# One core, streamed fp32 weights: reciprocal root rows inside a tile, two mixer tails in a new order, mLSTM gates as a full tile

## The chip, the core and the metric

The kernel runs on one core of a Trainium2 chip. The metric is the device time of one execution in microseconds (us); below it is the median of the runs shown. The profile is of one further execution.

The engines are called PE (TensorE, matmuls), DVE (VectorE), ACT (ScalarE), POOL (GpSimd) and SP (SyncE, which here only issues loads).

## The reference

A sequence of 256 tokens with 1024 features goes through six layers. The first two (`hybrid_layer`) project once, run three mixers side by side and project back. The other four are what the change is mostly about:

```python
def swiglu(x, w_gu, w_down):
    g, u = jnp.split(x @ w_gu, 2, axis=-1)
    return (jax.nn.silu(g) * u) @ w_down
...
for layer in range(4):
    g = norm_gains[layer]
    h = x + 0.5 * swiglu(rmsnorm_2(x, g[0]), w_ffn_gu[layer, 0], w_ffn_down[layer, 0])
    xn = rmsnorm_2(h, g[1])
    mix = hgrn2_mixer / mlstm_mixer / swa_mixer / hgrn2_mixer   # layer 0, 1, 2, 3
    h = h + mix(xn)
    h = h + 0.5 * swiglu(rmsnorm_2(h, g[2]), w_ffn_gu[layer, 1], w_ffn_down[layer, 1])
    gate = jax.nn.sigmoid(rmsnorm_2(h, g[3]) @ w_ple_gate[layer])
    x = h + gate * (p[layer] @ w_ple_proj[layer])
```

`rmsnorm_2` divides a token by the root of the mean of its squares and multiplies with a gain. An HGRN mixer has 8 heads of 128 and ends in: norm of each head, times `silu(og)`, times `w_out`. In layer 0 the lower bound `lb` of its forget gate is 0, in layer 3 it is not. The mLSTM mixer has 4 heads of 256 values; 8 gate columns `x @ w_if` (four input, four forget gates) go through `15 * tanh(gates / 15)` and a log-sigmoid; it ends in a norm of each head, times `sigmoid(og)`, times `w_out`. All is fp32.

## The kernel before

**Layout.** x lies transposed, features on the partitions: `x_res` is 128 x 8 tiles x 256 tokens. A product gives one PSUM tile of 128 outputs x 256 tokens.

**The stream of weights.** All weights come as 781 chunks of 128 x 1024 fp32 (`w_raw`), one for one output tile over all 8 feature tiles. SP issues their loads (L80) into 4 buffers. ACT rounds a chunk to the high part `w_hi` (L90, `hi_for`), DVE takes the difference, `w_lo` (L98, `lo_for`); both have 6 buffers. PE waits for a chunk (`wait_chunk`) and then makes three matmuls per feature tile j: L138 (high x high), L139 (high x `w_lo`), L144 (`xn_lo` x high), 24 in a tile. x is split the same way into `xn_hi` (L204 on ACT) and `xn_lo` (L209 on DVE).

**A norm without waiting.** The division by the root is put behind the product. While PE already multiplies the unscaled x, sums of squares are made (L366 on PE, `sum_squares`), their mean goes to SBUF (L379, ACT), POOL takes the power -1/2 (L393), PE spreads the result over 128 partitions by two transposes (L404, in `rstd_rows`), and DVE copies that to SBUF (L412, `take_rstd`). Only then can DVE scale the finished tiles (L536, L690, L982, L987) and free their PSUM banks. A section starts with a stretch in which two tiles run side by side, first all products with `xn_hi`, then those with `xn_lo` ("low phase"). `rstd_rows` stands in the third or fourth tile.

**PSUM.** Banks: `ps_gu` 0 and 1, four of `ps_acc`, `ps_sum`, `ps_misc`.

**Sections.** `ffn`: gate and up tiles in turn, `h = silu(g) * u` split by L519 and L545, then down products into `ps_acc`. `ple`: gate and projection. `project`: the input tiles of a mixer. `OutProjection`: y is split pair by pair (`split_hi` L1177, `split_lo` L1187); its first four output tiles are computed side by side as y comes (`place` gives their banks, so the four chunks are all needed early), the other four after that. Its `finish` adds each tile to x (L1271), and splits and squares the new x for the next section (L204, L209, L217; folds of squares L244, L248).

**The tails.** In `hgrn` the 8 head outputs lie in `ps_acc`; `head_norm` takes squares, their sums over partitions on PE into `ps_gu`, Ln and Exp, then DVE multiplies (L2355, L2360). Between them four gate tiles are projected into `ps_sum` and `ps_misc`, read by L982. `end_mixer` then gives the output product the banks `ps_gu` 0, `ps_gu` 1, `ps_sum`, `ps_misc`: the two last of them are free only after L982 has read the last two gate tiles. `mlstm` does the same with L3193, L3212, L3223, the sigmoid L3231 and its table load L3253.

**The forget gate with a bound** (`bounded`, layer 3): POOL does two operations for each of four heads (L2732, L2733), twice; the decays wait for the last.

**mLSTM gates.** The 8 gate columns are a first tile of another form: the weights' 8 columns are the moving side, tokens on the partitions (L153, L154, L158, 128 x 8 results, 48 matmuls), side by side with the first query tile. `gate_steps` places their small operations between the next tiles.

The order on each engine is the order in which the program writes it; there is no scheduler.

## Time and profile before

| | us |
|---|---|
| median of 3 runs | 2593.26 |
| lowest, highest | 2592.62, 2598.38 |
| the profiled execution, device time | 2591.68 |
| its span in the trace | 2589.7 |
| PE busy in it | 2515.2 |
| DVE, ACT, POOL busy | 1724.2, 1322.9, 97.3 |

Between the span and the time of the same execution lie 2.0 us. A bracket behind a row of a timeline, [2.41 <-DVE x_res L1271], is the time for which the engine had nothing to do before this instruction, and what ended it. The granted clock is given as a share of full speed. A tile of 24 matmuls at full clock takes 2.88 us, 0.12 us from one start to the next, though each matmul is listed with 0.28 us, since they overlap.

### The profile page before, as it was taken

To read this page: it belongs to the slowest core of one execution; us is meant where nothing else is said; L and a number is where in the kernel's file an instruction comes from. 1 tells how busy PE (TensorE), PEld (TensorE's weight loads), DVE (VectorE), ACT (ScalarE), POOL (GpSimd) and SP (SyncE) were. 2 spreads that over 40 slices of the span, in tenths; PEclk is the share of its full clock that TensorE was granted. 3 is DMA by queue.
4 is the path that set the end of the run, shared out by engine and by line. 5 is a ranking of instruction groups with operands and counts; after the bars stand their busy time and mean duration, and the time that the engine had idled before them with its cause. 6 is when DMAs were issued, how large, how long until landed. Compare 5 with 4: busy or idle time off the path is not lost.

```text
span 2589.7 us, 51722 instructions
## 1 busy us (share of the span) xinstructions
PE 2515.2 (97%) x20424; PEld 2478.8 (96%) x20424; DVE 1724.2 (67%) x2417; ACT 1322.9 (51%) x2019; POOL 97.3 (4%) x103
## 2 busy tenths in 40 slices
PE   7999999999999999999999999998999999999999
PEld 7999999999999999999899999987999999999999
DVE  7768757568665576566666675676666755767656
ACT  5745645446554464444444554465445544655444
POOL 1010010001100000000000000000000000220000
PEclk9999999999999999999999999999999999999999
DMA  7305306554355545555365555532555555435553
GB/s 259 123 34 171 123 33 212 186 179 163 122 171 186 181 162 190 183 158 175 115 198 182 172 178 186 180 125 87 188 182 167 187 185 182 161 122 171 180 186 122
DMA packets 115233, 418.85 MB, mean 162 GB/s; under 512 B 12816, under 2 KB 13968, under 8 KB 114832
## 3 DMA queue, kind: packets, MB, share of 16 engines
q1 hardware_dynamic: 114240, 413.10, 48.8%
q8 instruction: 108, 1.77, 0.3%
q0 software_dynamic: 560, 2.10, 0.3%
q10 hardware_dynamic: 288, 1.57, 0.2%
q14 instruction: 37, 0.30, 0.0%
HBM read 414.62 MB, written 2.10 MB: 161 GB/s over the span
## 4 chain that ended last, share of the span: by engine, by line
PE 82%; DVE 11%; ACT 3%; issue 2%; POOL 1%; DMA 0%; SPq 0%; DVEq 0%; ACTq 0%
PE ps_gu L138 15%; PE ps_gu L144 15%; PE ps_gu L139 15%; PE ps_acc L138 8%; PE ps_acc L144 8%; PE ps_acc L139 8%; DVE w_lo L98 3%; PE ps_acc L2590 1%; ACT w_hi L90 1%; PE ps_misc L138 1%; PE ps_acc L2148 1%; PE ps_misc L139 1%; PE ps_misc L144 1%; PE ps_sum L366 1%; DVE arena L1593 1%
## 5 line engine op out<-in xcount | busy, mean ns | idle before, releaser
L98 DVE TENSOR_TENSOR w_lo<-w_raw,w_hi 128x1024 fp32r<-128x1024 f32 x781 | 953.0, 1225 | 451.7 <-ACT w_hi L90 451.6
L138 PE MATMUL ps_gu<-xn_hi,w_hi 128*128 128x256 f32 x3840 | 1087.5, 286 | 25.7 <-DVE w_lo L98 12.1
L139 PE MATMUL ps_gu<-xn_hi,w_lo 128*128 128x256 f32 x3840 | 1077.9, 284 | 0.0
L144 PE MATMUL ps_gu<-xn_lo,w_hi 128*128 128x256 f32 x3840 | 1041.3, 284 | 0.0
L90 ACT ACTIVATE w_hi<-w_raw 128x1024 fp32r<-128x1024 f32 x781 | 819.9, 1054 | 417.4 <-PE ps_gu L144 305.3
L138 PEld LDWEIGHTS ps_gu<-xn_hi,w_hi 128*128 128x128 f32 x3840 | 738.7, 192 | 32.2 <-DVE w_lo L98 12.1
L139 PEld LDWEIGHTS ps_gu<-xn_hi,w_lo 128*128 128x128 f32 x3840 | 739.3, 193 | 0.3
L144 PEld LDWEIGHTS ps_gu<-xn_lo,w_hi 128*128 128x128 f32 x3840 | 717.1, 192 | 0.0
L138 PE MATMUL ps_acc<-h_hi,w_hi 128*128 128x256 f32 x1496 | 420.3, 281 | 1.2 <-DVE h_lo L545 1.2
L144 PE MATMUL ps_acc<-h_lo,w_hi 128*128 128x256 f32 x1496 | 420.3, 281 | 0.0
L139 PE MATMUL ps_acc<-h_hi,w_lo 128*128 128x256 f32 x1496 | 416.4, 278 | 0.0
L515 ACT ACTIVATE silu<-ps_gu 128x256 f32<-128x256 f32 x176 | 67.6, 384 | 456.0 <-DVE ps_gu L536 456.0
L138 PEld LDWEIGHTS ps_acc<-h_hi,w_hi 128*128 128x128 f32 x1496 | 281.9, 188 | 2.8 <-DVE h_lo L545 2.8
L139 PEld LDWEIGHTS ps_acc<-h_hi,w_lo 128*128 128x128 f32 x1496 | 281.9, 188 | 0.0
L144 PEld LDWEIGHTS ps_acc<-h_lo,w_hi 128*128 128x128 f32 x1496 | 280.7, 188 | 0.0
L536 DVE TENSOR_TENSOR ps_gu<-ps_gu,rstd 128x512 f32<-128x512 f32 x176 | 123.0, 699 | 85.9 <-PE ps_gu L144 85.6
L540 DVE TENSOR_TENSOR h<-silu,ps_gu 128x256 f32<-128x256 f32 x176 | 74.2, 421 | 89.9 <-ACT silu L515 89.9
L393 POOL TENSOR_TENSOR rstd_columns<-mean_square_columns,powers 128x2 f32<-128x2 f32 x17 | 14.2, 836 | 2029.6 <-ACT mean_square_columns L379 2029.6
L545 DVE TENSOR_TENSOR h_lo<-h,h_hi 128x256 fp32r<-128x256 f32 x176 | 73.7, 419 | 7.7 <-ACT h_hi L519 7.7
L519 ACT ACTIVATE h_hi<-h 128x256 fp32r<-128x256 f32 x176 | 71.8, 408 | 7.8 <-DVE h L540 7.8
L138 PE MATMUL ps_misc<-xn_hi,w_hi 128*128 128x256 f32 x232 | 67.6, 291 | 5.2 <-issue 3.2
L204 ACT ACTIVATE xn_hi<-x_res,vec 128x256 fp32r<-128x256 f32 x136 | 61.7, 497 | 21.2 <-DVE x_res L576 13.6
(452 smaller groups left out, 2751.2 us busy)
## 6 DMA issues: line engine op xcount, KB each, us to landing
w_raw<-in_w_dram SPq DMA_DIRECT2D x781, 512.0 KB, 4.1
const<-in_const_dram SPq DMA_DIRECT2D x1, 1280.0 KB, 10.3
x_res<-in_x_dram SPq DMA_DIRECT2D x2, 512.0 KB, 5.8
distance_rows<-arena POOLq DMA_DIRECT2D x1, 1024.0 KB, 6.3
p_all<-distance_rows POOLq DMA_DIRECT2D x2, 512.0 KB, 6.1
p_all<-in_p_dram ACTq DMA_DIRECT2D x1, 1024.0 KB, 6.6
...
```

The costliest lines, as they stand in the source:

```text
L90: act.activation(self.w_hi[:, s, :], self.w_raw[:, r, :], ACT.Copy).then_inc(self.w_hi_ready.sem, 1)
L98: dve.tensor_tensor(self.w_lo[:, s, :], self.w_raw[:, c % NR, :], self.w_hi[:, s, :], ALU.subtract)\
L138: pe.matmul(out, self.w_hi[:, s, j0:j0 + width], rhs_hi, start=start, stop=False, skip_group_check=True)
L139: pe.matmul(out, self.w_lo[:, s, j0:j0 + width], rhs_hi, start=False, stop=False, skip_group_check=True)
L144: return pe.matmul(out, self.w_hi[:, s, j0:j0 + width], rhs_lo, start=False, stop=last, skip_group_check=True)
L204: act.activation(self.hi[:, m, :], self.k.x[:, m, :], ACT.Copy, scale=self.gain[:, m:m + 1])\
L366: mm = pe.matmul(k.ps_sum[:, tt:tt + 1], k.xn[:, m, tt * P:(tt + 1) * P], k.ones[:, 0:1], start=(m == 0 and tt == 0), stop=(m == tiles[-1] ...
L515: act.activation(k.s[:, t % 2, :], k.ps_gu[t % 2][:, 0:S], ACT.Silu).then_inc(silu.sem, 1)
L519: act.activation(k.h_hi[:, t % 2, :], k.h[:, t % 2, :], ACT.Copy).then_inc(hh.sem, 1)
L536: dve.tensor_tensor(gu, gu, k.rstd[:, :].unsqueeze(1).to_broadcast([P, 2, S]), ALU.mult).then_inc(sc.sem, 1)
L540: dve.tensor_tensor(k.h[:, t % 2, :], k.s[:, t % 2, :], k.ps_gu[t % 2][:, S:2 * S], ALU.mult)\
L545: dve.tensor_tensor(k.h_lo[:, t % 2, :], k.h[:, t % 2, :], k.h_hi[:, t % 2, :], ALU.subtract)\
```

## The change

It has eight parts.

A. `ffn`: the two transposes of `rstd_rows` stand inside tile t = 1, n = 0, behind its fifth of eight products, not behind the whole tile. One kind of ffn (`inner`, before the first of the four layers) keeps its place.
B. `ple`: they stand ahead of tile m = 2, not behind its fifth product.
C. `project` with its own root, and the first tile of a `first_layer`: behind product j = 2, not j = 4.
D. `OutProjection.finish`: DVE adds the last two x tiles before it makes the last two `w_lo`; ACT likewise splits the last x tiles before the last `w_hi`.
E. `bounded`: the fourth head's two operations go from POOL to DVE.
F. `hgrn`'s tail is written out in `hgrn`; the gate tiles alternate with the norms in another order, and output tiles 2 and 3 go to the two `ps_acc` banks whose heads were normed first.
G. `mlstm`: the gate columns are a tile of the ordinary form (24 matmuls, 256 columns wide, padded weights). DVE scales it, then PE turns it by two transposes (`turn_gates`) in the fifth tile; `gate_steps` come one tile later.
H. `mlstm`'s tail: the sigmoid's table is loaded earlier, the last two gate tiles are read later (`later=True`), one chunk is split at a place of its own, and output tiles 2 and 3 go to the banks of the first two heads.

`head_norm`, which the first two layers still use, keeps only the case with two outputs.

```diff
@@ ffn
+                    if t == 1 and n == 0 and j == (KD - 1 if k.inner else 4):
+                        rstd_rows(k, pe)
                 mm.then_inc(k.chunk_done.sem, 1)
-                if t == 1 and n == 0:
-                    rstd_rows(k, pe)
@@ ple
+        rstd_rows(k, pe, n)
         for m in range(2, KD):
...
-                if m == 2 and j == 4:
-                    rstd_rows(k, pe, n)
@@ project
-                if with_rstd and t == 3 and j == 4:
+                if with_rstd and t == 3 and j == 2:
                     rstd_rows(k, pe)
+                if within and t == len(tiles) - 1 and j == 2:
+                    within(pe)
@@ OutProjection.finish, vector engine
+                if 0 < t < KD - 2:
                     k.lo_for(dve, c0 + t)
-                for n in {5: [0], 6: [1]}.get(t, []):
-                    nxt.fold_step(dve, n)
+                if t == 5:
+                    fold(dve, 0)
+            k.lo_for(dve, c0 + KD - 2)
+            fold(dve, 1)
             nxt.split_lo(dve, KD - 1)
-            nxt.fold_step(dve, 2)
+            fold(dve, 2)
+            k.lo_for(dve, c0 + KD - 1)
@@ first_layer
-            if j == 4:
+            if j == 2:
                 rstd_rows(k, pe)
@@ hgrn, bounded
-            for n in range(4):
+            for n in range(3):
                 pool.wait_ge(*at[n])
+                ins = factors(pool, 4 * g + n)
+        @block.vector
+        def _(dve):
+            dve.wait_ge(*at[3])
+            dve.wait_ge(*made("forget_ready"))
+            factors(dve, 4 * g + 3).then_inc(*up("forgets_ready"))
@@ hgrn, tail
+    sums(0)
+    sums(1)
+    for j in range(2):
+        normed(j)
+        gated(j, early)
+    g4 = gate_tile(4, k.ps_sum, side[0])
+    out.split_hi(0)
+    sums(2)
+    sums(3)
+    out.split_lo(0)
+    out.split_hi(1)
+    out.split_lo(1)
+    g5 = gate_tile(5, k.ps_misc, side[1])
+    gate_at = last_silu(2, [g4, g5])
+    normed(2)
+    normed(3)
+    g6 = gate_tile(6, k.ps_sum, [g4])
+    gated(2, gate_at)
+    g7 = gate_tile(7, k.ps_misc, [g5])
+    out.split_hi(2)
+    gate_at = last_silu(3, [g6, g7])
+    out.split_lo(2)
+    gated(3, gate_at)
+    out.split(3)
+    end_mixer(k, out, [(k.ps_acc[:, order[j], :], [norm_at[j]]) for j in range(2)])
@@ mlstm, gates
+    def turn_gates(pe):
+        pe.wait_ge(*gates_read)
+        for w in side:
+            pe.wait_ge(*w)
+        for tt in range(TT):
+            mm = pe.transpose(k.ps_misc[:, tt * P:(tt + 1) * P], den[:, tt * P:(tt + 1) * P], k.ident)
+        mm.then_inc(turned.sem, 1)
...
-    project(k, [("mul", True, 8, gates[:, 0:2, :])] + [("mul", False, P, m(q, h)) for h in range(H)],
-            first=True, with_rstd=True, beside=gate_steps)
+    project(k, [("mul", False, P, m(den, 0))] + [("mul", False, P, m(q, h)) for h in range(H)],
+            first=True, with_rstd=True, beside=gate_steps, within=turn_gates)
@@ mlstm, tail
+    g6 = gate_tile(6, k.ps_sum, g4, hi_done=True, later=True)
     normed(2, root1)
+    block.vector(lambda dve: k.lo_for(dve, c6))
     gated(2, gate_at)
+    g7 = gate_tile(7, k.ps_misc, g5, later=True)
     out.split_hi(2)
     out.split_lo(1)
+    gate_at = last_sigmoid(3, [g6, g7])
+    normed(3, root1)
+    block.vector(lambda dve: k.lo_for(dve, c6 + 1))
     out.split_lo(2)
+    gated(3, gate_at)
     out.split(3)
-    end_mixer(k, out)
+    end_mixer(k, out, [(k.ps_acc[:, j, :], [norm_at[j]]) for j in range(2)])
```

Three places in the order of instructions. The first is PE at the start of the first ple, at the end of the low phase. Before, word for word (three matmuls of tile m = 2 for each product; `ps_misc` is its bank, `ps_sum` takes the root rows):

```order
L138 MATMUL ps_misc<-xn_hi0,w_hi 128x256
L139 MATMUL ps_misc<-xn_hi0,w_lo 128x256
L144 MATMUL ps_misc<-xn_lo0,w_hi 128x256
L404 MATMUL ps_sum<-const,rstd_columns 128x128 x2
L138 MATMUL ps_misc<-xn_hi0,w_hi 128x256
L139 MATMUL ps_misc<-xn_hi0,w_lo 128x256
```

With the change:

```order
L144 MATMUL ps_gu0<-xn_lo0,w_hi 128x256
L144 MATMUL ps_gu1<-xn_lo0,w_hi 128x256
L404 MATMUL ps_sum<-const,rstd_columns 128x128 x2
L138 MATMUL ps_misc<-xn_hi0,w_hi 128x256
L139 MATMUL ps_misc<-xn_hi0,w_lo 128x256
L144 MATMUL ps_misc<-xn_lo0,w_hi 128x256
```

The two transposes moved from the middle of tile m = 2 to its front.

The second is DVE at the end of an output product (the last two additions to x, `ps_gu` 0 and 1), before:

```order
L209 SCALAR_TENSOR_TENSOR xn_lo0<-x_res,vec,xn_hi0 128x256
L98 TENSOR_TENSOR w_lo<-w_raw,w_hi 128x1024
L244 TENSOR_TENSOR xn<-xn 128x512
L1271 TENSOR_TENSOR x_res<-x_res,ps_gu0 128x256
L209 SCALAR_TENSOR_TENSOR xn_lo0<-x_res,vec,xn_hi0 128x256
L98 TENSOR_TENSOR w_lo<-w_raw,w_hi 128x1024
L248 TENSOR_TENSOR xn<-xn 128x512
L1271 TENSOR_TENSOR x_res<-x_res,ps_gu1 128x256
```

With the change:

```order
L209 SCALAR_TENSOR_TENSOR xn_lo0<-x_res,vec,xn_hi0 128x256
L98 TENSOR_TENSOR w_lo<-w_raw,w_hi 128x1024
L244 TENSOR_TENSOR xn<-xn 128x512
L1286 TENSOR_TENSOR x_res<-x_res,ps_gu0 128x256
L209 SCALAR_TENSOR_TENSOR xn_lo0<-x_res,vec,xn_hi0 128x256
L1286 TENSOR_TENSOR x_res<-x_res,ps_gu1 128x256
L209 SCALAR_TENSOR_TENSOR xn_lo0<-x_res,vec,xn_hi0 128x256
L98 TENSOR_TENSOR w_lo<-w_raw,w_hi 128x1024
```

The last addition (L1271, now L1286) stands three rows earlier, ahead of the sixth `w_lo` and the fold.

The third is DVE in mLSTM's tail, from the norm of the third head on, before (L982 reads a gate tile, L3212 and L3223 norm and gate a head, L1187 splits y, L2907 stands ahead of the output product):

```order
L3212 SCALAR_TENSOR_TENSOR xn<-ps_acc,vec,arena 128x256 x2
L3223 TENSOR_TENSOR xn<-xn,arena 128x512
L1187 TENSOR_TENSOR xn_lo1<-xn,xn_hi1 128x512
L982 TENSOR_TENSOR arena<-ps_sum,rstd 128x256
L98 TENSOR_TENSOR w_lo<-w_raw,w_hi 128x1024
L1187 TENSOR_TENSOR xn_lo1<-xn,xn_hi1 128x512
L3212 SCALAR_TENSOR_TENSOR xn<-ps_acc,vec,arena 128x256 x2
L982 TENSOR_TENSOR arena<-ps_misc,rstd 128x256
L98 TENSOR_TENSOR w_lo<-w_raw,w_hi 128x1024
L3223 TENSOR_TENSOR xn<-xn,arena 128x512
L1187 TENSOR_TENSOR xn_lo1<-xn,xn_hi1 128x512
L2907 COPY tiny<-xn 128x1
```

With the change:

```order
L982 TENSOR_TENSOR arena<-ps_sum,rstd 128x256
L3295 SCALAR_TENSOR_TENSOR xn<-ps_acc,vec,arena 128x256 x2
L98 TENSOR_TENSOR w_lo<-w_raw,w_hi 128x1024
L3306 TENSOR_TENSOR xn<-xn,arena 128x512
L982 TENSOR_TENSOR arena<-ps_misc,rstd 128x256
L1189 TENSOR_TENSOR xn_lo1<-xn,xn_hi1 128x512
L3295 SCALAR_TENSOR_TENSOR xn<-ps_acc,vec,arena 128x256 x2
L98 TENSOR_TENSOR w_lo<-w_raw,w_hi 128x1024
L1189 TENSOR_TENSOR xn_lo1<-xn,xn_hi1 128x512
L3306 TENSOR_TENSOR xn<-xn,arena 128x512
L1189 TENSOR_TENSOR xn_lo1<-xn,xn_hi1 128x512
```

The reads of the last gate tiles, `ps_sum` and `ps_misc`, stand among the same work, but the output product no longer takes these banks, and the two L98 no longer follow the reads directly.

## Rows read from the trace of the kernel before

**Rows 1.** The page, part 1: busy time, share of the span, instructions.

```profile
PE 2515.2 (97%) x20424; PEld 2478.8 (96%) x20424; DVE 1724.2 (67%) x2417; ACT 1322.9 (51%) x2019; POOL 97.3 (4%) x103
```

**Rows 2.** Waits of PE: engine, line, waited for: us, times, longest.

```profile
PE ps_gu L138 <- ACT silu L672: 5.9, 7, 1.4
```

**Rows 3.** Stretches: us, busy PE, PEld, DVE, ACT, POOL, clock, DMA share, GB/s.

```profile
592.10:597.86 5.76, 5.76 (x51) 5.76 (x49) 5.57 (x12) 5.76 (x10) 0.00 (x0) 1.00 0.00 0
597.86:604.45 6.59, 6.58 (x56) 6.37 (x54) 5.25 (x8) 1.65 (x4) 1.36 (x1) 1.00 0.45 143
1153.61:1163.32 9.71, 9.71 (x75) 9.71 (x74) 9.49 (x16) 6.06 (x10) 0.00 (x0) 0.83 0.08 18
1163.32:1171.40 8.08, 8.08 (x55) 7.98 (x55) 1.19 (x6) 2.16 (x3) 2.56 (x3) 0.78 0.47 176
712.23:728.01 15.78, 13.51 (x98) 13.10 (x97) 9.02 (x15) 6.22 (x8) 0.00 (x0) 0.89 0.31 101
2338.76:2353.04 14.28, 12.01 (x98) 11.60 (x97) 9.03 (x15) 6.21 (x8) 0.00 (x0) 1.00 0.34 112
1246.77:1266.80 20.03, 14.49 (x99) 14.08 (x97) 9.01 (x16) 6.39 (x9) 0.00 (x0) 0.83 0.23 80
```

**Rows 4.** Timeline, start of an ffn: start, us, engine, [idle].

```profile
747.14 0.69 POOL L393 TENSOR_TENSOR rstd_columns<-mean_square_columns,powers 128x2 f32<-128x2 f32 x1 [68.88 <-ACT mean_square_columns L379]
...
749.58 0.27 PE L404 MATMUL ps_sum<-const,rstd_columns 128*128 128x128 f32 x1
...
749.99 0.42 DVE L412 COPY rstd<-ps_sum 128x256 f32<-128x256 f32 x1 [0.73 <-PE ps_sum L404]
...
752.99 0.39 PE L138 MATMUL ps_acc<-h_hi,w_hi 128*128 128x256 f32 x1 [0.15 <-DVE h_lo L545]
```

**Rows 5.** Timeline, power in a mixer; start of a ple; chunk loads, all.

```profile
600.18 1.36 POOL L393 TENSOR_TENSOR rstd_columns<-mean_square_columns,powers 128x2 f32<-128x2 f32 x1 [189.27 <-ACT mean_square_columns L379]
...
938.91 3.74 SPq L80 DMA_DIRECT2D w_raw<-in_w_dram  x4
...
DMA to landing us min/median/max: 3.1/4.1/10.3
...
944.48 0.42 DVE L412 COPY rstd<-ps_sum 128x256 f32<-128x256 f32 x1 [2.34 <-PE ps_sum L404]
...
945.93 0.36 PE L138 MATMUL ps_gu<-xn_hi,w_hi 128*128 128x256 f32 x1 [0.41 <-ACT silu L672]
...
961.96 0.39 PE L138 MATMUL ps_gu<-xn_hi,w_hi 128*128 128x256 f32 x1 [1.41 <-ACT silu L672]
```

**Rows 6.** PE's waits at the starts of a mixer and a first layer.

```profile
604.85 0.35 PE L138 MATMUL ps_gu<-xn_hi,w_hi 128*128 128x256 f32 x1 [0.41 <-ACT arena L2704]
...
237.24 0.36 PE L138 MATMUL ps_gu<-xn_hi,w_hi 128*128 128x256 f32 x1 [0.77 <-DVE arena L982]
```

**Rows 7.** Timeline, end of an output product.

```profile
203.50 1.22 DVE L98 TENSOR_TENSOR w_lo<-w_raw,w_hi 128x1024 fp32r<-128x1024 f32 x1
...
205.23 0.41 DVE L1271 TENSOR_TENSOR x_res<-x_res,ps_gu 128x256 f32<-128x256 f32 x1
...
205.90 0.36 PE L138 MATMUL ps_gu<-xn_hi,w_hi 128*128 128x256 f32 x1 [2.41 <-DVE x_res L1271]
```

**Rows 8.** Timeline, the bounded forget gate; price of such a DVE operation.

```profile
2275.55 0.55 POOL L2732 TENSOR_SCALAR arena<-arena,bounds 128x256 f32<-128x256 f32 x1
2276.09 0.91 POOL L2733 TENSOR_SCALAR arena<-arena,bounds 128x256 f32<-128x256 f32 x1
...
2277.05 0.71 PE L2590 MATMUL ps_acc<-arena 128*128 128x128 f32 x4 [1.26 <-POOL arena L2733]
...
L3033 DVE TENSOR_SCALAR arena<-arena x4: 345/346/348, 1196.3 to 1199.2; 128x256 f32<-128x256 f32 x4
```

**Rows 9.** Timeline, mLSTM's tail.

```profile
1246.01 1.28 ACT L3253 ACT_TABLE_LOAD   x1
...
1253.42 0.55 PE L138 MATMUL ps_misc<-xn_hi,w_hi 128*128 128x256 f32 x1 [3.18 <-issue]
```

More of the change, by code:

```diff
@@ new lines, in gate_tile, with last_silu, _ @@
+    def gate_tile(h, ps, free):
+        return project(k, [("mul", False, P, m(gate, h))], banks=[(ps, free)])[0]
+    def last_silu(j, at):
+        @block.scalar
+        def _(act):
+            for w in at:
+                act.wait_ge(*w)
+            act.activation(bank_of(gate, j), bank_of(gate, j), ACT.Silu).then_inc(*up("gate_ready"))
+        return [made("gate_ready")]
+    side = [[k.side_read[n]] + [made(w) for w in ("misc_free", "y_ready", "sum_read", "rstd_ready")] for n in range(2)]
@@ L3244, in mlstm, with _ @@
     root1, free1 = roots(1)
+    @block.scalar
+    def _(act):
+        act.preload_act_table(ACT.Sigmoid)
     out.split_lo(0)
-    g5 = project(k, [last_gate(5)], banks=[(k.ps_misc, [misc_at])])[0]
+    g5 = gate_tile(5, k.ps_misc, misc_at)
+    gate_at = last_sigmoid(2, [g4, g5])
+    c6 = k.used
+    block.scalar(lambda act: k.hi_for(act, c6))
     normed(1, root0)
```

204 lines of the change are left out of this document (109 added, 95 removed).

## The prediction, made before the changed kernel was run

> **What bounds the kernel now.** I read the page first: PE is busy for 97% of the span, DVE for 67%, ACT for half [rows 1]. So only two things can shorten the run: fewer matmuls, or fewer and shorter waits of PE. The view of waits sorts PE's idle time by what ended it. What the reader is to see is that they are small and many: L672, say, seven waits of up to 1.4 us in the ple sections [rows 2]. Third come the stretches: the same piece of work at two places, or a piece against its matmul count, which shows what waits and what a lower granted clock cost together [rows 3]. Last, the timeline around each wait names what would be late next.
>
> A wait costs a little more than its bracket: the first matmul after it is listed with 0.36 us instead of 0.28, and the second weight load starts later too. From rows such as 205.90 [rows 7] I take 0.16 us for it, an estimate.
>
> The full-speed pace is 0.12 us a matmul: HGRN's first two tiles, 48 matmuls, take 5.76 us [rows 3].
>
> **A, ffn.** L404 runs at 749.58, DVE copies at 749.99, and the first down tile then waits 0.15 us for h [rows 4]. Three products, nine matmuls, are passed: 1.08 us earlier. The power ends at 747.14 + 0.69 = 747.83, the transposes would stand at 748.50, so PE doesn't wait for them (margin 0.67). DVE's copy now has a `w_lo` of 1.22 us in front of it, ending at about 749.25, so 0.8 us of the 1.08 arrive, more than the wait. Gain 0.15 + 0.16 = 0.31, in seven ffns of this kind: **2.2**. More than that is not to be had here.
>
> **B, ple.** DVE copies the root at 944.48, having waited for it; PE then waits 0.41 at 945.93 and, the chain still being late, 1.41 at 961.96 [rows 5]. Five products, 15 matmuls, are passed: 1.8 us earlier. But a full 1.8 is too much: the next chunks are issued from 938.91 on, four in 3.74 us (SP waits between them for free buffers), and at the median of 4.1 us to landing [rows 5] they come at about 943 to 947, an estimate; ACT and DVE split them in front of the later gates. The shift that arrives is between 0.57 (the first wait alone, 0.41 + 0.16) and 1.8; the two waits together with their restarts are 2.1. I take 1.56, because both waits lie on the same chain. In figures: 1.8 less 0.24, an estimate of what a gate that stands behind one split gives back. Three times: 4.7. The last ple has only its 0.41: 0.57. **5.25**, with ends 2.3 and 6.0.
>
> **C, project and first layer.** Six matmuls, 0.72 us. At 604.85 PE waits 0.41 for a bank, at 237.24 0.77 [rows 6]. HGRN's two starts and the second first layer get 0.72 each; the first one shows less, 0.3, swa's start hardly any, 0.1. **2.5**, ends 1.5 and 3.
>
> **D, finish.** The finished bank waits for x's last addition. PE stands 2.41 us until 205.90; DVE spent 203.50 to 204.72 on a `w_lo`, then on the fold, before the addition at 205.23 [rows 7]. The tile that it adds was complete at 203.5. With both behind it, the addition starts after the preceding split, 203.5, and the wait shrinks by 1.7. It gains only where the next section takes this bank at once, and of the eight output products that is one. **1.7**. What it costs: `w_lo` of the last two chunks comes 1.2 to 1.5 us later. They belong to the next section, whose stream is several chunks ahead there, so I count nothing (the fourth rival prices it).
>
> **E, bounded.** PE waits 1.26 until 2277.05 for POOL's last operation, which starts at 2276.09; a pair costs 0.55 + 0.91 on POOL. On DVE such an operation costs 0.35 [rows 8], a pair 0.7. The fourth head's pair is replaced, 1.46 by 0.7: 0.75, and 0.26 at the first group, whose wait is only 0.10: **1.0**, ends 0 (DVE behind a `w_lo`) and 1.8.
>
> **F, HGRN's tail.** The first output block is 4 tiles, 96 matmuls, 11.52 us at 0.12. It takes 15.78 in layer 0 and 14.28 in layer 3 [rows 3]: PE comes to the third and fourth bank, which wait for L982, and in layer 0 the granted clock then falls to half for 3.4 us (mean 0.89). With banks of heads that were normed long before, both waits go; PE then needs the third and fourth chunk, whose `w_lo` come 1.7 us before it. I take 4.1 of the 4.26 and 2.6 of the 2.76, since one restart remains: **6.7**.
>
> **G, gates.** The first two tiles take 9.71 us [rows 3], because 48 matmuls of 8 columns cost nearly a tile and a half, and the clock is at half for part (0.83 on average). Replaced by an ordinary tile they should take the 5.76 that HGRN's take in the same code: 3.95. In the next stretch, 8.08 against HGRN's 6.59: 1.5, since that is the same fall of the clock (0.78 and 1.00). The two transposes add 0.2, and nothing waits long for them: DVE's step moves by one tile, and the sums of log gates are needed 1.8 us after they come. **5.3**; if the clock falls anyway, 3.0.
>
> **H, mLSTM's tail.** The same block takes 20.03 us against 11.52. PE waits twice for reads of gate tiles, the longer time 3.18 at 1253.42, and the clock is at half for 6.8 us [rows 3, 9]. With the new banks both go, but PE now wants the fourth chunk at 1247.5, and its `w_lo` comes at about 1249.1: the table load of 1.28 us [rows 9] stands in front of the `w_hi`, and behind it DVE has head 3's norm. A new wait of 1.5, with restart 1.7, stays: 13.3 instead of 20.03. **6.7**; 5.1 if the clock falls at this wait, as it did in layer 0's HGRN tail but not in layer 3's. The trace shows both: the two HGRN tails have the same idle time of PE, 15.78 - 13.51 and 14.28 - 12.01, both 2.27, and the clock fell in one alone [rows 3].
>
> The sum is 2.2 + 5.25 + 2.5 + 1.7 + 1.0 + 6.7 + 5.3 + 6.7 = **31.4 us**. From the profiled execution's 2591.7 that gives 2560.3. It lies 1.6 under the median of the runs, so for the median **2561.9**, 1.2% faster.
>
> **A rule against the root rows' new places.** POOL's power takes 1.36 us in the mixer's start, while DVE makes `w_lo` after `w_lo` there (5.25 us busy in 6.59), and 0.69 in the ffn, ahead of DVE's next [rows 3 to 5]. The Trainium skill says in GPSIMD Engine Reference, section 1 (Specifications), that GpSimd's SBUF interfaces are shared with VectorE and that DVE instructions with two SBUF inputs contend with it. By that rule, the trace agrees. The margin of 0.67 in the ffn is all that the slowest power seen would use (1.36 - 0.69 = 0.67). By the rule, a power of 1.36 everywhere would cost nothing either, but leave no margin.
>
> **Rivals.**
> 1. Half of A to C is lost, 10% of D to H too, because the chunk stream, not the root, sets the pace at the starts (the loads of rows 5 are the sign). Gain 31.4 - 5 - 2 = 24.4: 2569.
> 2. The clock falls at the remaining waits: at mLSTM's tail (-1.6), in mLSTM's start (-2.3), and since everything shifts, at one or two attention waits more or less (1.7 each way). 31.4 - 3.9 - 1.7 = 25.8: 2567.5. For it: it is under 1.00 in four of the seven stretches [rows 3]. Against: the places with the longest waits go. The same with luck, two falls fewer, gives 2558.5.
> 3. More than expected: B to its end of 6.0, mLSTM's new wait hidden (1.7), two waits further on that vanish as the chain runs ahead: 2557.
> 4. Slower: the chunk stream. Each finish hands two `w_lo` on late, each tail reads y and chunks in a new order; at the eight section changes PE would have to wait for `w_lo`. It decides above 31.4 / 8 = 3.9 us for each, where DVE's part of a chunk costs 1.22 [rows 7]. At full price of 4.5 it gives 2598. Against: no such wait stands behind a finish now.
> 5. The change doesn't do what it says: the banks of the first heads aren't free in time, or L982 is still waited for by something behind it. F and H then fall to a third, 31.4 - 9 = 22.4: 2571.
>
> **Numbers.** Forecast 0.46, rivals 1 to 3 0.15, 0.14 and 0.10, rival 5 0.09, rival 4 0.02, and 0.04 for half of the gain or less, with its last quarter within 0.2%. About 0.2% (5 us) is what a measurement of this kernel can tell from no change. The range reaches from 2555, below rival 3, to 2572, above rival 5. Faster 0.96, within 0.2% 0.02, slower 0.02.
>
> **What would show it.** In the profile of the changed kernel: the stretches of the three output blocks at 11.7, 11.7 and 13.3 us (F, H), no L982 among the releasers of `ps_sum` and `ps_misc`; mLSTM's first two tiles in 5.8 us at clock 1.00 (G); ple's wait after its first tile gone and the one at its second section under 0.3 (B); no wait of PE for the power at L404 (A to C); the wait after the finish of the first layer down to 0.7 (D); L2590 waiting for DVE, under 0.6 (E). It is wrong if `w_lo` L98 becomes a releaser with more than 5 us in sum beyond the start of the program, or if the clock's falls are as many as before.

## The result, and the profile after

| | before | changed |
|---|---|---|
| median, us | 2592.94 (4 runs) | 2558.28 (4 runs) |
| lowest, highest | 2590.22, 2598.38 | 2556.86, 2560.62 |
| span of the profiled execution | 2589.7 | 2554.9 |

The changed kernel takes 0.9868 of the time before, 95% interval 0.9854 to 0.9882. The forecast was 2561.9 with a range of 2555 to 2572; the gain forecast was 31.4 us, the spans differ by 34.8.

The page of the changed kernel, part 1 (busy time and share of the span; compare [rows 1]): PE is busy for 17 us less, most of it because fewer matmuls run at half clock, and 18 us of waiting are gone. Windows of 2 us over both traces, up to 2545 us, find the clock at half for 41.0 us before and for 20.4 with the change. Half of the difference, 10.3 us, is the clock's share of the 34.8.

```profile
PE 2498.4 (98%) x20402; PEld 2466.5 (97%) x20402; DVE 1727.2 (68%) x2420; ACT 1324.0 (52%) x2021; POOL 95.7 (4%) x99
```

Its waits of PE (us in total, times, longest; compare [rows 2]). L672 of before is L671 here, L1271 is L1286. The new entry is the wait for a low part in `ps_acc`: mLSTM's tail.

```profile
PE ps_gu L138 <- ACT silu L671: 1.9, 3, 1.2
PE ps_acc L138 <- DVE w_lo L98: 1.4, 1, 1.4
PE ps_gu L138 <- DVE x_res L1286: 1.4, 2, 0.7
```

The stretches, columns as in [rows 3]: mLSTM's first two tiles and the next two, then the first output blocks of HGRN in layer 0, in layer 3, and of mLSTM.

```profile
1141.87:1147.62 5.75, 5.75 (x50) 5.75 (x49) 5.56 (x12) 5.75 (x10) 0.00 (x0) 1.00 0.02 4
1147.62:1154.05 6.43, 6.43 (x57) 6.43 (x56) 5.81 (x9) 2.24 (x4) 3.71 (x3) 1.00 0.43 128
707.07:718.64 11.57, 11.57 (x99) 11.51 (x97) 5.52 (x10) 2.96 (x5) 0.00 (x0) 1.00 0.42 138
2307.64:2319.21 11.57, 11.57 (x98) 11.51 (x97) 5.52 (x10) 2.97 (x5) 0.00 (x0) 1.00 0.42 139
1229.56:1242.79 13.23, 11.82 (x98) 11.56 (x97) 9.59 (x18) 4.82 (x7) 0.00 (x0) 1.00 0.46 154
```

They answer to 9.71, 8.08, 15.78, 14.28 and 20.03 us. All are at clock 1.00, and the two HGRN blocks contain no wait. With that, the signs that the prediction named for A, C, D and F to H have come. B's came in part, since its late wait was to be under 0.3 us (below), and for E PE no longer waits at all.

In the ples, the wait for the sigmoid after the first tile is gone and the late one is 0.40, 0.28 and 1.20 us, where each was 1.41 [rows 5]. At the end of the first layer's output product (timeline, DVE and PE; compare [rows 7]) the addition comes 1.2 us after the preceding one, not behind `w_lo` and fold:

```profile
200.91 0.42 DVE L1286 TENSOR_TENSOR x_res<-x_res,ps_gu 128x256 f32<-128x256 f32 x1
...
202.12 0.42 DVE L1286 TENSOR_TENSOR x_res<-x_res,ps_gu 128x256 f32<-128x256 f32 x1 [0.39 <-PE ps_gu L144]
...
202.80 0.35 PE L138 MATMUL ps_gu<-xn_hi,w_hi 128*128 128x256 f32 x1 [0.72 <-DVE x_res L1286]
```

To see where the time went I cut each trace at the starts of the POOL operation that ends a root (the power L393; in the ffn with `inner`, L335). They mark the same place of the program in every kernel. Lengths in us between them, without five ffns that repeat the pattern of A (each 0.3 to 0.4 shorter):

| from one root to the next | before | again | changed | again | third |
|---|---|---|---|---|---|
| first layer (C, D) | 192.74 | 194.26 | 189.16 | 189.12 | 189.12 |
| second layer (C) | 195.77 | 194.48 | 193.94 | 193.94 | 193.92 |
| ffn with `inner` (none) | 189.46 | 189.51 | 189.76 | 189.73 | 189.74 |
| HGRN, layer 0 (C, F) | 146.96 | 146.98 | 142.22 | 142.03 | 142.03 |
| ffn (A) | 193.65 | 193.68 | 193.31 | 193.31 | 193.23 |
| ple 1 (B) | 29.53 | 29.53 | 27.90 | 27.77 | 27.76 |
| ffn (A), mLSTM's start (G) | 196.78 | 196.96 | 190.98 | 190.96 | 190.97 |
| mLSTM (H) | 118.81 | 118.38 | 111.96 | 111.96 | 111.95 |
| ple 2 (B) | 29.53 | 29.55 | 27.77 | 27.86 | 27.77 |
| swa (none) | 109.80 | 109.45 | 109.43 | 109.58 | 110.50 |
| ple 3 (B) | 29.53 | 29.53 | 28.69 | 28.70 | 27.77 |
| HGRN, layer 3 (C, E, F) | 147.40 | 147.39 | 142.11 | 142.57 | 142.05 |
| all, first to last root | 2543.59 | 2543.62 | 2508.96 | 2509.38 | 2508.46 |

"Again" and "third" are the executions of the next section. Most sections repeat to 0.1 us, which is far finer than the medians. One reason is that they leave out the start of the program, where PE waits 12.1 us for its first low part in one trace and up to 14.2 in another. The rows where the same kernel differs from itself are the subject of the first experiment.

### The profile page after: what moved, and what is told of

It is laid out like the page before. It is cut to its first block, busy times and chain, and to the rows that moved or that the text cites. A ratio compares the mean times of both kernels' runs of the same rounds, so it can differ in the third digit from the quotient of the medians.

```text
span 2554.9 us, 51685 instructions
## 1 busy us (share of the span) xinstructions
PE 2498.4 (98%) x20402; PEld 2466.5 (97%) x20402; DVE 1727.2 (68%) x2420; ACT 1324.0 (52%) x2021; POOL 95.7 (4%) x99
## 4 chain that ended last, share of the span: by engine, by line
PE 85%; DVE 10%; ACT 3%; issue 2%; DMA 1%; SPq 0%; DVEq 0%; ACTq 0%
PE ps_gu L138 16%; PE ps_gu L139 16%; PE ps_gu L144 16%; PE ps_acc L138 8%; PE ps_acc L144 8%; PE ps_acc L139 8%; DVE w_lo L98 3%; PE ps_acc L2585 1%; DMA w_raw<-in_w_dram 1%; ACT w_hi L90 1%; PE ps_acc L2163 1%; ACT xn_hi L204 1%; PE ps_sum L366 1%; PE ps_misc L139 0%; PE ps_misc L138 0%
## 5 line engine op out<-in xcount | busy, mean ns | idle before, releaser
L98 DVE TENSOR_TENSOR w_lo<-w_raw,w_hi 128x1024 fp32r<-128x1024 f32 x781 | 954.5, 1227 | 429.5 <-ACT w_hi L90 429.0
L138 PE MATMUL ps_acc<-xn_hi,w_hi 128*128 128x256 f32 x320 | 92.5, 292 | 1.7 <-DVE w_lo L98 1.4
L139 PE MATMUL ps_acc<-xn_hi,w_lo 128*128 128x256 f32 x320 | 90.1, 285 | 0.0
L393 POOL TENSOR_TENSOR rstd_columns<-mean_square_columns,powers 128x2 f32<-128x2 f32 x17 | 15.0, 883 | 2000.9 <-ACT mean_square_columns L379 2000.9
L144 PE MATMUL ps_acc<-xn_lo,w_hi 128*128 128x256 f32 x320 | 84.7, 285 | 0.0
```

Source lines behind the costliest of these rows:

```text
L98: dve.tensor_tensor(self.w_lo[:, s, :], self.w_raw[:, c % NR, :], self.w_hi[:, s, :], ALU.subtract)\
L138: pe.matmul(out, self.w_hi[:, s, j0:j0 + width], rhs_hi, start=start, stop=False, skip_group_check=True)
L139: pe.matmul(out, self.w_lo[:, s, j0:j0 + width], rhs_hi, start=False, stop=False, skip_group_check=True)
L144: return pe.matmul(out, self.w_hi[:, s, j0:j0 + width], rhs_lo, start=False, stop=last, skip_group_check=True)
```

## Experiments

### Both kernels again: what belongs to the program, what to the execution

No edit. For the kernel before:

> The kernel before, unchanged, for the falls of TensorE's granted clock. In its first trace the clock is at half at 119, 310, 334, 716, 1160, 1252, 1737, 1751 and 1781 us; in the changed kernel's at 307, 403, 1710, 1723 and 1754. Theory: a fall follows the pattern of waits, so the same program shows the same nine again, and the 2.5 us that the first layers gave beyond my sum (119 and 334 gone, 403 new) belong to the change. Rival: in the first layers it is chance from one execution to the next: then this trace has other falls there, and those 2.5 us are no part of the change. Either way the waits themselves and the stretches at clock 1.00 repeat to 0.05 us.

For the changed kernel, twice:

> The changed kernel, unchanged, for the same question. Theory (pattern): falls at 307, 403, 1710, 1723 and 1754 again. Rival (chance): at least one of the two in the first layers is gone or another is there. The waits of the ple sections, 0.40, 0.28 and 1.20 us in the first trace of this kernel, are 0.2 to 0.5 in all three if the third was a late load by chance, and 1.2 again in the third if its place in the program makes it.

> The changed kernel, unchanged, to compare the other three with on the same chip: 0.987 of the kernel before, waits of 0.4, 0.3 and 1.2 us in the three ples if they belong to the program's places, and the clock's falls at 307 and 403 us again if they belong to the program.

The kernel before took 2591.87 us in its one run, the changed one 2558.55 in one and 2557.90 as a median of four (2556.73 to 2559.83; 0.9863, interval 0.9846 to 0.9879). The windows of the first trace of before (length, busy PE, PEld, DVE, ACT, POOL, granted clock, DMA share, GB/s):

```profile
119.00:122.40 3.40, 3.40 (x19) 3.40 (x18) 2.31 (x2) 1.60 (x2) 0.00 (x0) 0.50 0.02 5
207.40:210.80 3.40, 3.40 (x31) 3.40 (x30) 1.72 (x4) 0.05 (x1) 0.00 (x0) 1.00 0.83 246
310.20:313.50 3.30, 3.30 (x16) 3.30 (x17) 2.26 (x4) 2.99 (x8) 0.00 (x0) 0.50 0.00 0
```

and of its second trace:

```profile
118.70:122.00 3.30, 3.30 (x18) 3.30 (x17) 2.54 (x3) 1.90 (x3) 0.00 (x0) 0.50 0.02 5
207.40:210.70 3.30, 3.30 (x17) 3.30 (x17) 1.77 (x4) 0.10 (x1) 0.00 (x0) 0.50 0.69 202
310.20:313.50 3.30, 1.86 (x16) 1.89 (x17) 2.19 (x7) 2.78 (x9) 0.00 (x0) 1.00 0.00 0
```

The falls at 119 and 334 us repeat; the one at 310 is missing, and one at 207 is there instead, behind the wait for x at 205.96 us. A third execution of the same code, the first 700 us of the kernel with changed banks below, shows it at clock 1.00 at 120 and at half at 207, 313 and 408:

```profile
120.00:123.40 3.40, 3.40 (x31) 3.40 (x30) 2.36 (x4) 2.89 (x7) 0.00 (x0) 1.00 0.00 0
206.80:210.10 3.30, 3.30 (x18) 3.30 (x17) 2.64 (x5) 0.96 (x2) 0.00 (x0) 0.50 0.74 215
312.60:315.90 3.30, 3.30 (x18) 3.30 (x17) 2.54 (x3) 2.37 (x4) 0.00 (x0) 0.50 0.02 5
408.20:411.50 3.30, 3.30 (x18) 3.30 (x16) 1.23 (x1) 0.44 (x1) 2.68 (x6) 0.50 0.86 319
```

So in the first layers chance decides between executions of one program where the clock falls, and its first two sections (192.28 and 194.31 in that third execution) spread over 194.26 - 192.28 = 2.0 us and 195.77 - 194.31 = 1.5 us. In the changed kernel the falls at 307 and 403 came back in all three executions (first trace):

```profile
307.00:310.30 3.30, 3.30 (x18) 3.30 (x16) 2.47 (x3) 2.66 (x6) 0.00 (x0) 0.50 0.00 0
402.60:405.90 3.30, 3.30 (x18) 3.30 (x17) 1.23 (x1) 0.74 (x1) 2.91 (x6) 0.50 0.53 175
```

Three kernels below with the same code up to there fell at about 120 and 331 instead. The rival holds for the places of the falls, but not for their number. Over all traces of this study, up to the first of the four layers:

| code of the first layers | traces | falls in each | first three sections together, us |
|---|---|---|---|
| before, without C and D | 4 | 3 | 576.3 to 578.3, mean 577.6 |
| with C alone (the root rows alone) | 1 | 3 | 577.3 |
| with C, D undone in the changed kernel | 1 | 2 | 575.7 |
| changed, C and D | 8 | 2 | 572.8 to 574.0, mean 573.2 |

The first traces of the two kernels differ by 5.1 us in these three sections, where my sum had 2.7 for them (D 1.7, C 1.0); the question above calls the rest 2.5. The means differ by 4.3. So about 1.6 of it comes again and again with the changed code, about the price of one fall, and the rest, 0.8, is the luck of the pair of executions. Which part of the change takes the third fall away is not shown: with C but not D there were three falls in one kernel and two in another.

The third ple is a second case of chance: 28.69, 28.70, 27.77 us. In the slow ones ACT stands idle for a weight load at its start, in the fast one it doesn't (ACT, the changed kernel's first execution, and below it the third):

```profile
1979.09 1.06 ACT L90 ACTIVATE w_hi<-w_raw 128x1024 fp32r<-128x1024 f32 x1 [2.62 <-DMA w_raw<-in_w_dram]
```

```profile
1979.36 1.06 ACT L90 ACTIVATE w_hi<-w_raw 128x1024 fp32r<-128x1024 f32 x1 [1.70 <-PE ps_gu L144]
```

### The new banks alone

The edit, in the kernel before (`acc_by` makes the next user of the `ps_acc` banks wait for the additions):

```diff
-    out.place([(k.ps_gu[n], [k.gu_read[n]]) for n in range(2)] +
-              [((k.ps_sum, k.ps_misc)[n], [...]) for n in range(2)])
+    out.place([(k.ps_gu[n], [k.gu_read[n]]) for n in range(2)] + banks)
...
-    k.gu_read, k.side_read, k.slot = read[0:2], read[2:4], 0
+    k.gu_read, k.slot = read[0:2], 0
+    k.acc_by += read[2:4]
```

> The kernel before, with one thing of the change: output tiles 2 and 3 of the HGRN and mLSTM tails go to the banks of the first two heads. The order of the work is the old one. First output blocks before: 15.78, 14.28 (HGRN), 20.03 us (mLSTM); with the whole change 11.5, 11.5 and 13.1. If the banks were the cause, the blocks are 11.6, 11.6 and 13 to 14, and 13 us are gained. My theory after reading both traces: the order matters at least as much, since the old one makes the fourth chunk's low part only at 712.5 to 713.7 and 1250.4 to 1251.6, where PE wants it at 712.7 and 1247.4: blocks of 12.6, 12.6 and 16 to 17.5, a gain of 7.4 us in all (5 to 9).

Measured: 2586.91 us against 2592.33 (0.9981, interval 0.9971 to 0.9990), 5.4 us. The three output blocks (HGRN, mLSTM, HGRN, in the columns of before):

```profile
712.86:725.33 12.47, 11.82 (x98) 11.55 (x97) 9.03 (x15) 6.23 (x8) 0.00 (x0) 1.00 0.41 128
1245.76:1263.06 17.30, 13.29 (x98) 13.03 (x97) 9.01 (x16) 6.41 (x9) 0.00 (x0) 0.90 0.28 93
2334.75:2347.22 12.47, 11.82 (x99) 11.55 (x97) 9.03 (x15) 6.23 (x8) 0.00 (x0) 1.00 0.40 128
```

As my second theory had it: 12.47, 12.47 and 17.30. The banks alone bring a little over half of the effect. PE now waits for the fourth chunk's low part. The time shows 5.4 us where the blocks give 7.85 (sum below): the other differences lie outside them, 1.6 us more at mLSTM's start, where the clock is at half for longer, among them.

### The new order with the old banks

The reverse of that edit, in the changed kernel.

> The changed kernel, with one thing of it undone: the output tiles 2 and 3 of the HGRN and mLSTM tails are in ps_sum and ps_misc again, so they wait for the last gate tiles' reads. If the banks are most of it, 8 us or more come back. My theory: the new order reads ps_sum early and ps_misc at 707.3 to 707.7, where PE comes to it at 707.4, and in the mLSTM at 1232.3 to 1232.7, 0.9 us after the low part that PE waits for anyway: blocks of 12.0, 12.0 and 14.3, 2 us slower than the changed kernel.

Measured: 2561.62 us (0.9886, interval 0.9869 to 0.9902), 3 us slower than the changed kernel. Its blocks:

```profile
706.41:718.05 11.64, 11.64 (x99) 11.56 (x97) 5.52 (x10) 2.96 (x5) 0.00 (x0) 1.00 0.42 137
1228.83:1244.30 15.47, 13.09 (x98) 12.85 (x97) 9.59 (x18) 4.82 (x7) 0.00 (x0) 0.89 0.38 132
2310.56:2322.20 11.64, 11.64 (x99) 11.56 (x97) 5.53 (x10) 2.97 (x5) 0.00 (x0) 1.00 0.43 138
```

In HGRN the banks give 11.64 - 11.57 = 0.07 us once the order is new: the last gate tiles are read before PE comes. In the mLSTM the block is 2.24 us longer, 1 us of wait for `ps_misc` and the rest a fall of the clock behind it (mean 0.89). Neither half alone reaches the whole: banks alone 15.78 + 14.28 + 20.03 - 42.24 = 7.85 us in the three blocks, order alone 50.09 - 38.75 = 11.34, both 50.09 - 36.37 = 13.72. They overlap, so undoing one says little of its worth. Layer 3, where the clock falls in neither kernel, shows the parts without it: 1.81 us for the banks, 2.64 for the order, 2.71 for both. In layer 0 a fall of the clock, about 1.5 us, is in each of the three numbers, and the next experiment loses that fall without touching the tail.

### The root rows alone

A, B and C as in the diff, in the kernel before.

> The kernel before with parts A, B and C alone: the root rows at their new places in ffn, ple, project and first layer, nothing else. Theory: each section gives what it gave in the changed kernel, since nothing there is shared with the tails: A 7 x 0.35 = 2.5, B 1.6 + 1.8 + 0.8 + 0.6 = 4.8, C 1.8, together 9.1 us (7.5 to 10.5, as the third ple's wait may be 0.3 or 1.2). Rival: part of it is only handed on to the next section, whose chunks aren't there sooner: then the starts are faster but the sum is under 6 us, and PE waits for low parts L98 more often than before.

Measured: 2585.63 us against 2592.69 (0.9968, interval 0.9957 to 0.9980), 7.1 us, a little under the 7.5 to 10.5 expected. Its sections: ffn 193.30, 193.23, 193.29, 193.23; ples 27.75, 29.00, 27.82. Each gives what it gives in the whole change (but for the second ple, where 0.53 of 1.76 arrives). HGRN in layer 0 is 144.85, 2.1 less, of which 1.6 is that its tail no longer falls (a window over that tail, clock 1.00, with the same waits as before):

```profile
710.00:726.00 16.00, 13.73 (x113) 13.39 (x112) 10.74 (x17) 7.45 (x9) 0.00 (x0) 1.00 0.35 117
```

Against that, swa's section is 111.52 instead of 109.80, and mLSTM's start 198.10 instead of 196.78, both by more time at half clock, at places that this kernel doesn't touch. The rival was wrong about the cause: no wait for L98 was added (2.5 and 2.0 us, as before). The gain isn't handed on; the clock takes and gives 1 to 2 us at other places. Why it does so isn't shown. For HGRN's tails the traces can be counted: the old tail shows a fall in four of eight passages (two tails in each of the four traces that have it), with the same 2.27 us of idle time, and the tail in the new order in none of 18 (nine traces).

### The gate columns alone

G as in the diff, in the kernel before.

> The kernel before with part G alone: the gate columns as an ordinary tile, turned by two transposes in the fifth. Theory: the fall of the clock at 1160 us belongs to the narrow matmuls and goes with them. The stretch of the first two tiles is 5.8 instead of 9.7 us and the next about 6.7 instead of 8.1, 5.3 to 5.6 us in all; of this 2.3 are the form of the matmuls (9.71 less half of the 3.28 us at half clock, less 5.76) and 3.1 the clock. Rival: the clock falls there anyway, since it follows the end of the ffn and not the form: then 2.3 us are gained.

```profile
1153.47:1159.22 5.75, 5.75 (x50) 5.75 (x49) 5.56 (x12) 5.75 (x10) 0.00 (x0) 1.00 0.02 4
1159.22:1165.79 6.57, 6.57 (x56) 6.41 (x55) 5.23 (x8) 2.49 (x4) 3.71 (x3) 1.00 0.47 147
```

The two stretches take 5.75 and 6.57 us, 5.5 less than 9.71 + 8.08, at clock 1.00 both: the fall belongs to the narrow matmuls. All other traces agree. In the four with the narrow matmuls the clock is at half there for about 7 us in two and about 10 in two, in the ten with the ordinary tile never. The kernel takes 2587.75 us against 2592.69 (0.9978, interval 0.9968 to 0.9989), 4.9 us; 1.8 us are lost again in HGRN's second tail (149.18 instead of 147.40), where the clock fell in this kernel and didn't before.

### The fourth head on POOL again

```diff
-            for n in range(3):
+            for n in range(4):
...
-        @block.vector
-        def _(dve):
-            dve.wait_ge(*at[3])
-            dve.wait_ge(*made("forget_ready"))
-            factors(dve, 4 * g + 3).then_inc(*up("forgets_ready"))
```

> The changed kernel with part E undone: POOL again does the fourth head's two operations. In the second HGRN's span from its power to the second tail the change gave 1.9 us more than before (31.11 less 29.25 us of lead), where I had 1.0. Theory: all 1.9 are E's: the pair on POOL took 1.46 where DVE takes 0.76, and the waits of 1.26 and 0.10 with their restarts (1.42 + 0.26) go, so this kernel is 1.7 to 1.9 us slower than the changed one, with PE waits for POOL of about 1.3 and 0.1 again. Rival: part of it is that the slow POOL operation (2.43 us before, 1.43 in the changed kernel, while DVE makes a low part) came out shorter by chance: then the waits return to under 1.0 and 0.8 to 1.2 us are lost.

Measured: 2560.41 us (0.9868, interval 0.9852 to 0.9885), 2.5 us over the changed kernel on that chip, and 143.93 in the section where that has 142.05: 1.88 us. The theory holds. The changed kernel, POOL and DVE in the second group of heads:

```profile
2240.32 1.43 POOL L2724 TENSOR_SCALAR arena<-arena,bounds 128x256 f32<-128x256 f32 x1
2241.73 1.07 POOL L2723 TENSOR_SCALAR arena<-arena,bounds 128x256 f32<-128x256 f32 x1
...
2245.24 0.41 DVE L2723 TENSOR_SCALAR arena<-arena,bounds 128x256 f32<-128x256 f32 x1 [1.02 <-POOL arena L2724]
2245.57 0.35 DVE L2724 TENSOR_SCALAR arena<-arena,bounds 128x256 f32<-128x256 f32 x1
```

and with the pair on POOL, POOL and PE:

```profile
2244.18 2.42 POOL L2728 TENSOR_SCALAR arena<-arena,bounds 128x256 f32<-128x256 f32 x1
...
2250.98 0.38 PE L2585 MATMUL ps_acc<-arena 128*128 128x128 f32 x1 [1.27 <-POOL arena L2728]
```

What I had missed is POOL's first L2724. It took 2.43 us in the traces of before and 2.42 here, but 1.43, followed by an L2723 of 1.07 where that had 0.55, in all executions with three heads on POOL. DVE's rows show what lies beside it. Before (POOL with them):

```profile
2269.93 0.89 DVE L2573 TENSOR_TENSOR arena<-arena 128x512 f32<-128x512 f32 x1
2270.27 2.43 POOL L2733 TENSOR_SCALAR arena<-arena,bounds 128x256 f32<-128x256 f32 x1
2270.76 1.23 DVE L98 TENSOR_TENSOR w_lo<-w_raw,w_hi 128x1024 fp32r<-128x1024 f32 x1
```

and in the changed kernel:

```profile
2240.33 0.70 DVE L2568 TENSOR_TENSOR arena<-arena 128x512 f32<-128x512 f32 x1
2240.96 1.41 DVE L98 TENSOR_TENSOR w_lo<-w_raw,w_hi 128x1024 fp32r<-128x1024 f32 x1
```

Before, POOL's operation starts 0.34 us behind a DVE operation on two SBUF tensors and lasts until 0.7 us after the low part that follows it. In the changed kernel both start together, POOL is done after 1.43 us, and the low part takes 1.41 instead of 1.23. Why DVE stands later against POOL with part E wasn't tested. The chain is shorter by the pair (1.46 - 0.76 = 0.7) and by this 0.48, and with the restart the whole wait of 1.27 and the 0.10 of the first group go.

### The old finish

D undone, in the changed kernel: both `finish` halves as before.

> The changed kernel with part D undone: the last two low parts ahead of x's last addition again, in all output products. Theory: only the first product gains by D; the wait of 0.72 at 202.8 us is 2.4 again, 1.7 us, and nothing moves at the other seven. Rival: D makes low parts 1.2 to 1.5 us late at the other products and costs something there, hidden in the sum: then the later sections of this kernel are shorter than the changed kernel's by 0.2 us or more each.

Measured: 2561.21 us (0.9870, interval 0.9853 to 0.9886). PE waits 2.46 us at 206.07 again, 1.74 more than 0.72; the first layer's section is 192.34, of which 1.5 is a fall of the clock at 207 behind that wait. All later sections are within 0.1 us of the changed kernel's, but for the two that vary by themselves (swa and the third ple) and the ffn with `inner` (189.47, no fall at 403). In none of these sections do the late low parts cost anything.

### The table load behind the split

```diff
-    @block.scalar
-    def _(act):
-        act.preload_act_table(ACT.Sigmoid)
     out.split_lo(0)
     g5 = gate_tile(5, k.ps_misc, misc_at)
+
+    @block.scalar
+    def _(act):
+        act.preload_act_table(ACT.Sigmoid)
```

> The changed kernel with one thing moved: in the mLSTM's tail the sigmoid's table load (1.28 us) stands behind the split of the fifth gate tile's chunk, not ahead of it. PE now waits 1.41 us at 1231.85 for a low part that DVE makes late, having stood idle 2.38 us for ACT's high part until 1226.80. Theory: that idle time is the table load's, everything behind it on DVE comes 1.28 us sooner, the sigmoid itself at the same time as now (it waits for the same table), and the first output block takes 11.6 to 11.9 instead of 13.1 us: 1.3 us faster than the changed kernel. Rival: DVE waits next for the high part of the sixth chunk or the sigmoid, and the block stays above 12.5.

DVE and PE in the changed kernel, ahead of the one wait left in the tail:

```profile
1226.80 1.22 DVE L98 TENSOR_TENSOR w_lo<-w_raw,w_hi 128x1024 fp32r<-128x1024 f32 x1 [2.38 <-ACT w_hi L90]
...
1231.85 0.39 PE L138 MATMUL ps_acc<-xn_hi,w_hi 128*128 128x256 f32 x1 [1.41 <-DVE w_lo L98]
```

and DVE with the load moved, and the stretch of the block:

```profile
1226.70 1.22 DVE L98 TENSOR_TENSOR w_lo<-w_raw,w_hi 128x1024 fp32r<-128x1024 f32 x1 [0.96 <-ACT w_hi L90]
...
1230.88:1242.70 11.82, 11.82 (x99) 11.56 (x97) 8.18 (x15) 3.42 (x6) 0.00 (x0) 1.00 0.42 135
```

DVE's idle time falls from 2.38 to 0.96 us, and the block takes 11.82 instead of 13.23 us; mLSTM's section is 110.55 instead of 111.96. The theory holds. The kernel takes 2557.70 us (0.9864, interval 0.9848 to 0.9880); against the changed kernel's 2558.28 and 2557.90 the medians don't resolve 1.4 us.

### The sigmoid first

```diff
-            if m < KD - 1:
+            if 2 <= m < KD - 1:
                 k.hi(act, c0 + 3 + m + AHEAD)
...
             act.activation(k.s[:, m % 2, :], out(m), ACT.Sigmoid).then_inc(*gate.up())
+            if m < 2:
+                k.hi(act, c0 + 3 + m + AHEAD)
```

and DVE's `w_lo` of these two behind the addition to x.

> The changed kernel with one thing moved: in ple, for the first two gate tiles ACT takes the sigmoid before it makes the next chunk's high part, and DVE makes the low part after the addition to x. PE's waits for L671 are 0.40, 0.28 and 1.20 us, once near the end of each of three ples. Theory: they are the lateness of one weight load (landed 4.4 to 6.6 us after its issue at a ple's start), handed from gate tile to gate tile by the order high part, sigmoid; with the sigmoid first they go, with restarts 0.56 + 0.44 + 1.36 = 2.4 us. Rival: the low parts that come later now (1.5 to 2 us) make PE wait for L98, or the wait returns because each later tile still has the old order: then under 0.5 us or slower.

Measured: 2566.84 us (0.9898, interval 0.9881 to 0.9914), 8.5 us slower. The theory was wrong, and of the rival only that the kernel could be slower came true: PE waits for no low part in the ples, but 2.3 us for the sigmoid late in each. The ples take 31.07, 30.34 and 31.10 us; behind that wait the clock falls in the first and the third, not in the second. DVE, first ple:

```profile
938.80 0.42 DVE L691 TENSOR_TENSOR ps_gu<-ps_gu,rstd 128x256 f32<-128x256 f32 x1
941.02 0.48 DVE L209 SCALAR_TENSOR_TENSOR xn_lo<-x_res,vec,xn_hi 128x256 fp32r<-128x256 f32 x1 [1.79 <-ACT xn_hi L204]
```

DVE stands idle 1.79 us for `xn_hi`, which ACT splits only behind the high part that the sigmoid was moved ahead of, and it never wins that back, since DVE is busy without a pause in a ple: scaling, low part, `xn_lo`, product and addition start every 2.65 us, against 2.88 for a tile on PE. A lateness at the start shrinks by 0.23 us a tile, 1.4 in six (worked out from the two periods). This is my explanation of why a root that comes 1.8 us sooner moved the ple's last wait by only 1 us and more; no run changed DVE's period to test it.

### Additions on POOL, and the table load

In addition to the moved table load:

```diff
+    @block.gpsimd
+    def _(pool):
+        for m in range(6):
+            pool.wait_ge(*prod.at(r0 + m + 1))
+            pool.tensor_tensor(k.x[:, m, :], k.x[:, m, :], k.h[:, m % 2, :], ALU.add).then_inc(xr.sem, 1)
...
-            dve.wait_ge(*prod.at(r0 + m + 1))
-            dve.tensor_tensor(k.x[:, m, :], k.x[:, m, :], k.h[:, m % 2, :], ALU.add).then_inc(xr.sem, 1)
+            if m >= 6:
+                dve.wait_ge(*prod.at(r0 + m + 1))
+                dve.wait_ge(*after[m - 1])
+                dve.tensor_tensor(k.x[:, m, :], k.x[:, m, :], k.h[:, m % 2, :], ALU.add).then_inc(xr.sem, 1)
```

> The changed kernel with the table load of the mLSTM's tail behind the chunk's split (as in table_later), and in each ple the first six additions to x on POOL, not on DVE. In a ple DVE works without a pause, 2.65 us for a tile (scaling, low part, x_lo, product, addition), where PE takes 2.88: a lateness at the start shrinks by only 0.23 us a tile, and the kernel with the sigmoid first was 2.5 to 3 us slower in each ple because it put idle time into that chain. Theory: with 2.2 us a tile the lateness is gone after two or three tiles, and PE's waits of 0.40, 0.28 and 1.20 us too, 2.4 us with restarts; with the 1.4 of the table 3.8 us faster than the changed kernel. Rival: POOL's addition takes over 1 us beside DVE and delays x, or slows DVE: the waits stay, and only the table's 1.4 are gained.

Measured: 2555.36 us (2555.10 to 2556.07; 0.9851, interval 0.9834 to 0.9867), against 2557.90 for the changed kernel on the same chip: 2.5 us in the medians, though the intervals of the ratios overlap; it is the fastest kernel of this study. The ples take 27.60, 27.60 and 28.06 us, so POOL gives only 0.17 in a quiet ple (27.77). POOL and DVE in the first ple:

```profile
938.83 0.74 POOL L685 TENSOR_TENSOR x_res<-x_res,h 128x256 f32<-128x256 f32 x1 [1.89 <-DVE h L705]
...
939.01 1.64 DVE L98 TENSOR_TENSOR w_lo<-w_raw,w_hi 128x1024 fp32r<-128x1024 f32 x1
```

The addition takes 0.74 us on POOL, and the low part beside it takes 1.64 instead of 1.22. The 0.42 us taken off DVE are given back; its period is 2.63, not 2.2. The rival was right that DVE is slowed, and wrong in its two other points: the addition takes 0.74 us, not over 1, and PE's waits for the sigmoid don't stay. They are gone in all three ples, and a wait of 0.27 to 0.34 us for `xn_hi` (L204), 3 to 4 us later, stands in their place. Since the changed kernel waits only 0.27 us in a quiet ple, little is left to gain there.

## Why the prediction was right, point by point

Measured are differences of the sections and stretches above, first trace against first trace. Where two parts share a section, A is taken as 0.4 us and F to H from their stretches. C's 1.9 hold 0.3 for the first layer as forecast, since its traces don't separate it; the last row is what is left of the 34.8 us by which the spans differ.

| part | forecast, us | measured |
|---|---|---|
| A, seven ffns | 2.2 | 2.6 |
| B, four ples | 5.25 | 4.9 |
| C, project, first layer | 2.5 | 1.9 |
| D, finish | 1.7 | 1.7 |
| E, bounded | 1.0 | 1.9 |
| F, HGRN's tails | 6.7 | 6.9 |
| G, gates | 5.3 | 5.5 |
| H, mLSTM's tail | 6.7 | 6.8 |
| the rest, nearly all in the first layers | 0 | 2.6 |
| sum | 31.4 | 34.8 |

A, D, G and H. The steps held, mechanism and size. H's new wait was forecast as 1.5 and is 1.41 us; that the table load is its cause was argued then and is shown now by moving it. H read the row of 3.18 us as a wait for the read of a gate tile, though the row names no releaser; the new banks alone take this wait and its neighbour of 2.4 us away, which shows it. G's whole is shown by the part alone; its split into 2.3 for the form and 3.1 for the clock is worked out from the time at half clock.

F was right in size and only partly in its mechanism. Its step was that with the banks both waits go. The banks alone leave blocks of 12.47 us, since the old order makes the fourth low part too late; the order alone, with the old banks, gives 11.64, all but 0.07 of the 11.57. So the order, which F's steps don't price, is enough in HGRN, and the banks are not. In mLSTM both are needed.

B. The step "1.8 less 0.24" gave 1.56 for each of three ples; measured are 1.63, 1.76 and 0.84, and 0.84 was a late load (1.76 in the third execution). The reason for the shortfall was only half right: it is the load in the bad case, but in the good ones, as far as the rows show, DVE's period of 2.65 us against PE's 2.88.

C was the term sized too high. I gave three starts the full 0.72. Measured are 0.5 in HGRN's first start, 0.4 in the second layer and 0.7 in HGRN's second start (0.5 there with the root rows alone, 147.40 against 146.93). The step that failed is that the wait at 237.24 shrinks with the root; it is 0.76 us in the changed kernel as it was 0.77, so it hangs on something else than the root's place. What, I didn't test.

```profile
233.72 0.35 PE L138 MATMUL ps_gu<-xn_hi,w_hi 128*128 128x256 f32 x1 [0.76 <-DVE arena L982]
```

E was the term sized too low: 1.0 against 1.88. It counted the pair, 0.75, and left out that an earlier POOL operation could get shorter too, by 0.48, and the restarts.

The 2.6 us beyond the terms are the granted clock's for the most part. The second rival had this mechanism with both signs, 1.7 us each way. Its lucky case, two falls fewer, gave 34.8 us, the very number measured. What came is one fall fewer in the first layers, in all eight traces of the changed code, and about 0.8 us of luck in the pair of traces compared. So the total lies nearer to this lucky case than to the forecast, and well inside the range.

The other rivals failed by their own tests: no wait for `w_lo` was added but the one foreseen (rival 4, and the old finish), at their new places the root rows waited nowhere for POOL (the rule on the shared interfaces), the half lost of A to C (rival 1) isn't seen, L982 released no bank of the tails (rival 5), and of rival 3 neither B's end of 6.0 nor a hidden wait in mLSTM came.
